# Gate rows by way of DRAM, and the first two up tiles by token halves, at the head of a feed-forward stage

## What is computed

```python
x  = x + g1 * (o @ w_out)                      # g1, g2: one number for each feature
h2 = modulate(rmsnorm(x, norm_ffn), sh2, sc2)
a, g = split(h2 @ w_up, 2)                     # 2816 channels each, 22 tiles of 128
x  = x + g2 * ((a * gelu(conv3x3(g) + conv_b)) @ w_down)
```

## Time and profile before

| | |
|---|---|
| device time, median of 3 runs | 1802.89 us (1802.82 to 1805.06) |
| span of the profiled execution, first to last instruction | 1795.7 us |
| time of the profiled execution itself | not given on the page |
| TensorE busy | 1744.2 us, 97% of the span |
| VectorE, ScalarE, GpSimd busy | 70%, 52%, 27% |
| mean granted TensorE clock | 0.994 of full speed |
| chain of work that ended last | 84% on TensorE, 6% VectorE, 4% ScalarE |

### The profile page before, as it was taken

The page is one execution under the profiler, slowest core; times in us unless marked ns, Lnnn a source line. Parts: engine busy times, 40 slices in busy tenths (PEclk is TensorE's granted clock), DMA queues, the critical chain, the costliest instruction groups (busy, mean ns, idle before and its releaser), DMA issues.

```text
span 1795.7 us, 33010 instructions
## 1 busy us (share of the span) xinstructions
PE 1744.2 (97%) x11190; PEld 1547.2 (86%) x11190; DVE 1251.2 (70%) x2359; ACT 942.1 (52%) x1389; POOL 492.9 (27%) x225
## 2 busy tenths in 40 slices
PE   9999989999999999999999999999999999999997
PEld 6799878897878999999999988888888787669996
DVE  4567587876424499067777578888888896667777
ACT  5466577544555544567777643333333575334444
POOL 4246744401568588800000000000000100013332
PEclk9999999999999999999999999999999999999999
DMA  6654443577344478755565687677767783355553
GB/s 216 200 188 141 166 152 118 190 248 266 121 164 150 135 222 228 228 179 172 174 173 173 195 263 239 235 235 236 237 239 236 272 276 122 113 176 187 183 183 113
DMA packets 122839, 347.63 MB, mean 194 GB/s; under 512 B 13904, under 2 KB 46800, under 8 KB 122512
## 3 DMA queue, kind: packets, MB, share of 16 engines
q1 hardware_dynamic: 121248, 339.52, 58.1%
q0 software_dynamic: 1520, 7.21, 1.1%
HBM read 328.84 MB, written 17.83 MB: 193 GB/s over the span
## 4 chain that ended last, share of the span: by engine, by line
PE 84%; DVE 6%; ACT 4%; issue 2%; POOL 2%; DMA 1%; POOLq 0%; DVEq 0%; ACTq 0%
PE banks L934 83%; POOL weight_rest L851 2%; ACT arena L1676 2%; DMA weight_ring<-in_stream 1%; ACT weight_high L1676 1%; PE banks L945 1%; DVE weight_rest L2307 1%; ACT span_exponentials L1676 0%; DVE arena L3110 0%; DVE arena L2991 0%; DVE arena L2348 0%; ACT scratch L1676 0%; ACT L1676 0%; DVE arena L2347 0%; DVE arena L2345 0%
## 5 line engine op out<-in xcount | busy, mean ns | idle before, releaser
L1676 ACT ACTIVATE weight_high<-weight_ring 128x1024 fp32r<-128x1024 f32 x448 | 473.0, 1057 | 453.4 <-PE banks L934 350.4
L851 POOL TENSOR_TENSOR weight_rest<-weight_ring,weight_high 128x1024 fp32r<-128x1024 f32 x165 | 414.4, 2521 | 264.5 <-ACT weight_high L1676 155.0
L2307 DVE TENSOR_TENSOR weight_rest<-weight_ring,weight_high 128x1024 fp32r<-128x1024 f32 x283 | 346.1, 1224 | 156.3 <-ACT weight_high L1676 153.4
L934 PE MATMUL banks<-a_high,weight_high 128*128 128x256 f32 x1216 | 304.0, 288 | 0.2 <-ACT weight_high L1676 0.2
L934 PE MATMUL banks<-a_rest,weight_high 128*128 128x256 f32 x1216 | 297.8, 283 | 0.0
L934 PEld LDWEIGHTS banks<-a_high,weight_high 128*128 128x128 f32 x1216 | 232.6, 191 | 1.5 <-issue 1.1
L934 PEld LDWEIGHTS banks<-a_rest,weight_high 128*128 128x128 f32 x1216 | 232.9, 192 | 0.3 <-issue 0.2
L934 PE MATMUL banks<-weight_high,gated_high 128*128 128x512 f32 x512 | 201.4, 393 | 0.0
L934 PE MATMUL banks<-weight_high,gated_rest 128*128 128x512 f32 x512 | 200.2, 391 | 0.0
L934 PE MATMUL banks<-a_high,weight_rest 128*128 128x256 f32 x1216 | 170.9, 283 | 2.4 <-POOL weight_rest L851 2.4
L934 PE MATMUL banks<-x_high,weight_high 128*128 128x256 f32 x672 | 167.5, 287 | 4.7 <-DVE x_rest L3079 3.7
(11 more groups left out here) (360 smaller groups left out, 3101.5 us busy)
## 6 DMA issues: line engine op xcount, KB each, us to landing
weight_ring<-in_stream SPq DMA_DIRECT2D x512, 512.0 KB, 3.5
arena<-in_stream SPq DMA_DIRECT2D x66, 512.0 KB, 3.3
unit_spill<-small SPq DMA_DIRECT2D x128, 128.0 KB, 3.6
scratch<-unit_spill SPq DMA_DIRECT2D x128, 128.0 KB, 3.2
residual<-in_x SPq DMA_DIRECT2D x2, 512.0 KB, 4.1
arena<-in_mem POOLq DMA_DIRECT2D x2, 512.0 KB, 5.3
arena<-in_ctx POOLq DMA_DIRECT2D x2, 512.0 KB, 4.8
arena<-in_keys POOLq DMA_DIRECT2D x1, 1024.0 KB, 5.2
```

The costliest lines, as they stand in the source:

```text
L851: nc.gpsimd.tensor_tensor(w_lo[:, e % 2, :], raw(e)[0], w_hi[:, e % 2, :], ALU.subtract).then_inc(S["rest_ready"], 1)
L934: return nc.tensor.matmul(out, lhsT, rhs, start=start, stop=stop, skip_group_check=True)
L1676: return nc.scalar.activation(out, in_, f, **kw)
L2307: tt(w_lo[:, e % 2, :], raw(e)[0], w_hi[:, e % 2, :], ALU.subtract).then_inc(S[ready], 1)
```

## The change

The gates' diagonals, spreading products, copies and the zero products go. VectorE adds the bias to both gates' columns earlier (`GATE_COLUMNS`, 16 numbers on each partition); GpSimd writes these to DRAM and loads them back as rows on all partitions, into another part of the arena.

The first two up tiles (`g0`, `a0`) are done in token halves, in products of 128 columns. The first half stands before the second half's transposes. One idle product follows it (its result is overwritten), and three more stand after the second transposes. The first down tile starts its sums anew instead of adding to zeros, so the loop's first turn is written out on TensorE. The two weights that the first half needs are loaded behind ring tile 11, split by ScalarE before the first half's features, and their rests made by VectorE before it turns to these features. GpSimd makes one more weight rest, and VectorE the first hidden tile's rest. The bank list changes with it. In it, job `w2` 1 1 moves from bank 4 to bank 5, and with the gate jobs gone the jobs `x3T` 0 0 and 0 1 come to banks 4 and 5.

```diff
     B.job("w2", 0, 0)
     B.job("o", 1)
-    for r in range(2):
-        B.job("gb", r)
     B.job("w2", 1, 0)
...
     for h in range(2):
         B.job("x3T", 0, h)
-    B.job("w2", 1, 1, bank=4)
-    for r in range(2, 4):
-        B.job("gb", r, bank=3 + r)
+    B.job("w2", 1, 1, bank=5)
+    B.job("g0", bank=4)
+    B.job("a0", bank=6)
...
     B.job("x3T", 1, 0, bank=7)
-    B.job("x3T", 1, 1, bank=4)
-    B.job("g0", bank=4)
-    B.job("a0", bank=6)
+    B.job("x3T", 1, 1, bank=5)
...
+                if sec == "out2" and i == 11:
+                    sp.wait_ge(S["rows_used"], 1)
+                    sp.wait_ge(S["z_made"], TT * N_MADE)
+                    for s in range(2):
+                        sp.dma_start(FR[:, s, :], stream[FFN0 + s]).then_inc(ffn_loaded[s], 16)
...
-            sp.wait_ge(S["rows_used"], 1)
-            for s in range(FRING):
+            for s in range(2, FRING):
...
+            pool.wait_ge(S["gates_summed"], 2)
+            with nc.allow_non_contiguous_dma("one number of each feature"):
+                pool.dma_start(gate_rows.rearrange("g k p -> p (g k)"), GATE_COLUMNS).then_inc(in_second, 16)
+            freed(pool, ("tot",))
+            pool.wait_ge(S["log_lo_ready"], TT)
+            pool.wait_ge(in_second, 5 * 16)
+            pool.dma_start(GB.rearrange("p g d -> p (g d)"),
+                           gate_rows.rearrange("g k p -> (g k p)").partition_broadcast(P)).then_inc(in_second, 16)
+            pool.wait_ge(in_second, 6 * 16)
...
-            hidden_rest(("a0",), 0, 0)
+            pool.wait_ge(S["hi_ready"], F0 + 4)
+            pool.wait_ge(S["hi_begun"], F0 + 3)
+            pool.wait_ge(S["ffn_lo_ready"], 3)
+            nc.gpsimd.tensor_tensor(w_lo[:, 1, :], raw(F0 + 3)[0], w_hi[:, 1, :],
+                                    ALU.subtract).then_inc(S["ffn_lo_ready"], 1)
...
             projected_half(1, 1)
-            gates_spread(1)
-            pe.wait_ge(S["zeros_ready"], 1)
-            for t in range(TT):
-                for h in range(2):
-                    mm(claim(("f", t, h)), ident, ZEROS, start=True, stop=False)
+            def channels_by_tokens(r, job, t):
+                e, s = F0 + r, tsl(t)
+                if t == 0:
+                    b = claim(job)
+                    pe.wait_ge(S["hi_ready"], e + 1)
+                else:
+                    b = bank(job)
+                for k in range(KC):
+                    ins = mm(b[:, s], w_hi[:, e % 2, hsl(k)], x3_hi[:, k, s], start=(k == 0), stop=False)
+                    if k == 0 and t == r:
+                        ins.then_inc(S["hi_begun"], 1)
+                    ins = mm(b[:, s], w_hi[:, e % 2, hsl(k)], x3_lo[:, k, s], start=False, stop=False)
+                if t == 1:
+                    ins.then_inc(S["hi_used"], 1)
+                else:
+                    pe.wait_ge(S["ffn_lo_ready"], r + 1)
+                for k in range(KC):
+                    ins = mm(b[:, s], w_lo[:, e % 2, hsl(k)], x3_hi[:, k, s], start=False, stop=(k == KC - 1))
+                if t == 1:
+                    filled(ins, job)
...
+            first_channels(0)
+            idle = claim(("f", 0, 0))
+            mm(idle, ident, const[:, 0:512])
             normed_turned(1)
+            for _ in range(3):
+                mm(idle, ident, const[:, 0:512])
+            first_channels(1)
...
             row_root(8, 0, "x3_ready")
-            x3_high(0)
             for r in range(2):
                 split_high(F0 + r)
+            x3_high(0)
             row_root(8, 1, "x3_ready")
             x3_high(1)
-            gates_spread(1)
...
+            split_high(F0 + 2, rests=(S["ffn_lo_ready"], 1))
             ffn_gate(("g0",), 0, 0)
-            split_high(F0 + 2, rests=(S["ffn_lo_ready"], 1))
...
             for t in range(TT):
                 if t == 0:
-                    for r in range(2):
-                        freed(dve, ("gb", r))
+                    dve.wait_ge(in_second, 6 * 16)
                 for b in range(2):
                     add_gated(("w2", b, t), 0, T2[:, 2 * t + b, :], b, t, "x3_ready")
                 row_mean(8, t)
+                row_scaled(8, t)
                 if t == 0:
-                    gate_diagonals(1, 40)
-                row_scaled(8, t)
+                    for r in range(2):
+                        e = F0 + r
+                        dve.wait_ge(S["hi_ready"], e + 1)
+                        tt(w_lo[:, e % 2, :], raw(e)[0], w_hi[:, e % 2, :],
+                           ALU.subtract).then_inc(S["ffn_lo_ready"], 1)
                 x3_features(t)
...
+            split_rest(F0 + 2, "ffn_lo_ready")
             conv_channels(("g0",), 0, n0, 0)
-            split_rest(F0 + 2, "ffn_lo_ready")
-            split_rest(F0 + 3, "ffn_lo_ready")
             hidden_channels(("a0",), 0, 0, second=False)
+            dve.wait_ge(S["hidden_made"], 1)
+            freed(dve, ("a0",))
+            tt(hidden_lo[:, 0, :], HF, hidden_hi[:, 0, :], ALU.subtract).then_inc(S["hidden_ready"], 1)
```

More of the change, by code:

```diff
@@ L543, in build @@
             g_k g_kd g_H z_made dve_columns ctx_e o_root v_ms v_root rows_used v_ready
-            oc_ready gdiag x3_ready ffn_center ffn_gelu x4_ready out_ready act_step dve_step zeros_ready warm_zeros
+            oc_ready gates_summed x3_ready ffn_center ffn_gelu x4_ready out_ready act_step dve_step warm_zeros
             neg_a m_hi_ready m_lo_ready at_hi_ready at_lo_ready y_hi_ready y_lo_ready mg_hi_ready
@@ L720, in build @@
         T512 = area(22528, 4, 512)
-        GB = area(24576, 2, D)
-        GBD = [area(22528, KC, P), area(26624, KC, P)]
+        GB = area(13312, 2, D)
+        gate_rows = nc.dram_tensor("gate_rows", [2, KC, P], F32).ap()
         T2 = area(20480, 4, 512)
@@ L732, in build @@
         smx = sb("softmax_stats", [P, TT, 4, 8])
+        GATE_COLUMNS = smx[:, 0, 0:2, :].rearrange("p a b -> p (a b)")
         warmed = sb("warmed", [P, 16])
@@ L762, in build @@
         TOTE = modsb[:, 32:40]
-        ZEROS = area(29696, 512)
-        WARM = ZEROS
+        WARM = area(29696, 512)
         by_head = lambda ap: ap.rearrange("p (h d) -> p h d", d=SP_)
@@ L1409, in _, with split_sums @@
                     units(U_EARLY + U_GATED + j, ("u3", j), i)
-            def split_sums(e, name, hi, lo_, turn, n, rest_ready, rest_count, last=False):
+            def split_sums(e, name, hi, lo_, turn, n, rest_ready, rest_count, last=False, first=False):
                 def high(w):
@@ L1415, in high @@
                         for h in range(2):
-                            o = bank((name, t, h))
-                            ins = mm(o, hi[:, tsl(t)], w[:, h * 512:(h + 1) * 512], start=False, stop=False)
+                            o = claim((name, t, h)) if first else bank((name, t, h))
+                            ins = mm(o, hi[:, tsl(t)], w[:, h * 512:(h + 1) * 512], start=first, stop=False)
                             if t == h == 0:
@@ L1580, in _ @@
             levels(1, 1)
[L1582 to L1587, removed]
             def mixed_turned(t):
@@ L1622, in _, with first_channels @@
             projected_half(1, 1)
-            gates_spread(1)
-            pe.wait_ge(S["zeros_ready"], 1)
-            for t in range(TT):
-                for h in range(2):
-                    mm(claim(("f", t, h)), ident, ZEROS, start=True, stop=False)
+            def channels_by_tokens(r, job, t):
[18 more added lines that the diff above has]
+                    filled(ins, job)
+            def first_channels(t):
+                pe.wait_ge(S["x3_hi_ready"], 2 * t + 2)
+                pe.wait_ge(S["x3_lo_ready"], 2 * t + 2)
+                for r, job in enumerate((("g0",), ("a0",))):
+                    channels_by_tokens(r, job, t)
+            first_channels(0)
+            idle = claim(("f", 0, 0))
+            mm(idle, ident, const[:, 0:512])
             normed_turned(1)
+            for _ in range(3):
+                mm(idle, ident, const[:, 0:512])
+            first_channels(1)
             def channels(r, job, count, turn=None):
@@ L1633, in channels, with down @@
                                count if turn is None else turn * 4 + count)
-            def down(r, c, par, turn=None):
+            def down(r, c, par, turn=None, first=False):
                 n = 0 if turn is None else turn * 2
@@ L1638, in down @@
                 split_sums(F0 + r, "f", hidden_hi[:, par, :], hidden_lo[:, par, :], turn, 6,
-                           S["ffn_down_lo_ready"], n + (c + 1))
+                           S["ffn_down_lo_ready"], n + (c + 1), first=first)
             def down_by_tokens(e, c, par):
@@ L1654, in down_by_tokens @@
                         filled(mm(bank(("f", t, h)), x_hi, wl[:, h * 512:(h + 1) * 512], start=False), ("f", t, h))
[L1656 to L1660, removed]
+            for u in range(2):
+                channels(2 + 3 * u, ("ga", 2 * u), 3 + 2 * u)
+                channels(3 + 3 * u, ("ga", 2 * u + 1), 4 + 2 * u)
```

(18 more changed lines are left out.)

4 lines of the change are left out of this document (removed).

## The result

| | before | after |
|---|---|---|
| device time, median | 1802.62 us (1799.59 to 1806.23) | 1807.87 us (1799.10 to 1813.68) |
| ratio, 95% interval | | 1.0027 (1.0016 to 1.0039) |
| span of the profiled execution | 1795.7 us | 1805.4 us |
| its own time | not given | 1807.16 us |
| mean granted clock | 0.994 | 0.990 |

The change is slower by 0.27%, 4.9 us by the ratio. I forecast 1803.5 and no change, with a range that ended at 1807.0; the result lies above it.

A forecast was written before the change was run, and what follows sets the result against it. TensorE, busy 97% of the span, was taken as the bound. The terms -1.72 + 2.45 + 1.72 + 1.09 - 1.94 - 1.01 gave +0.6 us, so 1803.5 us, no change, with a range from 1798.8 to 1807.0.

The forecast's parts named there:

- gate products out: First pair of gate-spreading products on TensorE goes; all up to the first token half's transposes slides: -1.72 us.
- bank wait, with late tiles: Before the last projection half, TensorE waits on bank 5 for VectorE's first-half features: +2.45 us, nothing added for late tiles.
- clock, last projection; first half for filler: Low clock behind the bank wait, +1.72 us; first narrow set and idle product replacing gates and zeros, +1.09.
- second half: Second token half's up tiles: 48 narrow products at full clock take 5.38 us for 7.32: -1.94.
- first half turn of the loop: Loop's first half turn, rests made earlier, no wait: 8.51 us for 9.52, -1.01.
- Gate rows: GpSimd's write and load through DRAM, covered by some 50 us, 40 left for the write: cost taken as nothing.
- What VectorE must do before: Two weight rests ahead of the first-half features; VectorE free between 1573.2 and 1575.4, wanted at 1574.95: nothing taken.
- the two tiles land late: Rival: the two up tiles arrive late for VectorE's rests, up to +3.5 us, 1807.0 in all; chance 0.10.
- The narrow products: Up tiles in token halves: 48 products of 128 columns at 0.112 us each, 5.38 us a set.
- cost by their columns: Rival for the up tiles' narrow products: 0.060 us each, -3.9 us in all, 1799.0; chance 0.18.
- cost like plain ones: Rival for the up tiles' narrow products: 0.224 us each, 10.75 a set, +11.3, 1814.2; chance 0.15.
- a gap of some 1.3 us, short of any that dropped the clock: Before the second half's first narrow product: three idle products leave this gap, and full clock is assumed behind it.

The follow-up runs named there:

- second experiment: The change with its two up tiles loaded behind ring tile 7 instead of 11, bank kept: 1803.60 us, ratio 1.0006 against the kernel before.
- the change's second trace: The change run once more, unchanged: 1808.87 us, ratio 1.0025 against the kernel before.
- the two experiments that take one of them away from the change: The change with whole up tiles after the second transposes and five idle products ahead: 1802.87 us; the change with five idle products behind the second transposes: 1803.07 us.
- the first two experiments: The change with the last projection half on bank 7: 1800.34 us; the change with its two up tiles loaded behind ring tile 7: 1803.60 us.
- the last experiment: The kernel before with three idle products behind its second transposes, nothing else: 1800.64 us, ratio 0.9992 against the kernel before.
- the bank alone: The change with the last projection half on bank 7 and the second half's transposes on banks 5 and 7: 1800.34 us, ratio 0.9985 against the kernel before.

## Why the prediction was wrong

Step by step, along the stretch (predicted, then the profile of after):

| step | predicted | measured |
|---|---|---|
| gate products out | -1.72 | -1.72 |
| bank wait, with late tiles | +2.45 | +4.26 |
| clock, last projection; first half for filler | +1.72 + 1.09 = +2.81 | +2.86 |
| second transposes to first product | 0 | +0.05 |
| second half | -1.94 | +1.52 |
| first half turn of the loop | -1.01 | +0.36 |
| sum | +0.59 | +7.33 |

**Gate rows: right.** GpSimd's timeline of after:

```profile
1509.43 1.21 POOL L906 DMA_DIRECT2D gate_rows<-softmax_stats  x1 [83.00 <-DVE softmax_stats L2990]
...
1520.50 0.55 POOL L910 DMA_DIRECT2D arena<-gate_rows  x1 [9.85 <-DMA gate_rows<-softmax_stats]
```

VectorE's timeline, the first gated sum:

```profile
1564.40 0.68 DVE L3079 TENSOR_TENSOR arena<-banks,arena 128x512 f32<-128x512 f32 x1
```

The write of 2048 single numbers, which I had bounded at 40 us, is followed by the load at 1520.50, some 11 us after its own issue (1.21 + 9.85). The load landed 4.8 us after issue, so the rows lay ready near 1525. VectorE first multiplies by them at 1564.40, some 39 us later, and doesn't wait. The cover is real.

**The bank wait: right in place, mis-sized.** TensorE stands where I put it and for the reason given; the step that failed is "What VectorE must do before", which took nothing for late tiles. I sized the landing from ring tiles at 4.4 us and from up tiles at 6.6, and took the middle; the two landed 7.1 and 7.9 us after issue. VectorE's timeline of after:

```profile
1576.74 2.49 DVE L3120 TENSOR_TENSOR weight_rest<-arena,weight_high 128x1024 fp32r<-128x1024 f32 x2 [4.54 <-ACT weight_high L1711]
1579.15 2.63 DVE L3101 TENSOR_SCALAR act_feature_major<-banks,modulation_sums 128x128 f32<-128x128 f32 x8
```

VectorE stood idle for 4.54 us until the first rounding was done, and could begin its features only at 1579.15, though the transposes ended at 1577.75 (1576.71 + 1.04). This cost +1.81: the rival "the two tiles land late", to which I gave 0.10, at about half its upper price. With 7.9 us in place of the middle, the prediction's own chain gives the same: 1566.6 + 7.9 + 1.06 + 1.18 is 1576.7, 1.8 after the 1574.95 at which the features want VectorE. Issued four tiles earlier (second experiment), the same wait is 2.30.

**The clock in the last projection: right.** It fell, as in four of the six waits before, and 2.86 for that step and the next together stands against 2.81. That the size fits is partly luck: in the change's second trace, where the clock stayed low until 1591, the same two steps cost +4.21.

**The narrow products: right.** 0.111 us against 0.112 taken; the row of plain products was the one to trust. The Trainium skill (TensorE: Matmul & The Clock Gate, section Back-to-back issue gap) has about 81 ns for 128 columns; no stretch here shows it for the rounded type, and the measurement decides. Two rivals fall with this, "cost by their columns" and "cost like plain ones". It also means that a narrow product costs almost what a wide one does (0.111 against 0.120), so halving a tile by tokens doubles its work: two sets of 48 take 10.7 us where the whole takes 5.8, and what they can hide is 4.28 us of norm.

**The second half and the first half turn: wrong in sign.** The step that failed is the sentence that leaves "a gap of some 1.3 us, short of any that dropped the clock". The wait was 1.20, as forecast. I had looked at long waits alone as what drops the clock, and had not asked what runs behind a short one. The trace of before couldn't have told me: nine of its waits on TensorE last 1.01 to 1.71 us, the granted clock is 1.00 in the 4 us behind each, and none of them stands before products of 128 columns. With the clock held, both terms come out (5.38 us in the second experiment, whose whole stretch is the forecast's); with the fall they give +1.88 instead of -2.95, 4.83 us between them. Without the second fall the stretch of after would be some 54.35, +2.5; with it +7.3; the timed median shows +4.9. That it lies between because some executions have the fall and others don't is argued, not shown: no trace says which of the timed ones had it.

**The rival on the other side** that I had priced highest, narrow products like plain ones, is not what happened. What did happen stood in the text as two small cases: late tiles, and a clock that I gave one price only in one place.

## What to carry to other kernels

When a list of banks or buffers shifts, look up for every job who held its bank last, and when its reader is done: three entries of that list, and what followed from them, were worth 7.5 us here (1807.87 against 1800.34), more than the 6.9 us of products that the change takes out (1.72 + 5.15). In these traces a wait's length alone didn't settle the clock; ask what stands behind it too, and close short waits ahead of work in small pieces. Before splitting a product by columns, compare the durations of the narrow and the wide one in the trace: where they are near, the split pays for all its work twice.

## What I had not expected of the hardware

**Behind a short wait before narrow products the clock fell, in some traces.** Over the eleven traces, a wait of 1.20 us followed by 48 narrow products was followed by a fall to 0.50 (1.2 GHz) in three of five; narrow products with no wait ahead held 1.00 in both; whole tiles behind a wait of 1.16 held it in all three. That it takes both, the wait and the narrow products, fits all ten of these, and the medians of the two experiments that take one of them away from the change; ten traces don't prove it. The first narrow set never lost it. Once low, it stayed so for 10.2 us in after (1603.1 to 1613.3), with TensorE busy throughout. What decides between executions of one kernel wasn't found, nor whether the fall is rarer in the first two experiments than in the change, as their narrower ranges (7.2 and 3.5 us, against 14.6) and their lower medians let one think.

**One execution's span is a poor base.** The same code ahead of the change ends its mixing at 1558.68 us in the trace of before and at 1561.27 in the last experiment's, and over all twelve traces up to 1566.12 (the bank alone): more than the terms argued over here. Most of this is the clock: ahead of the stretch it was low for 10.2 us in the trace of before and for 23.9 us in that of the bank alone, which at half speed is 6.8 of the 7.44 us between them. The stretch cut at the first and the last row that the change can move could be compared: the second experiment's came out 0.03 us from the forecast.
